# The second half of each turned key page is saved by VectorE instead of ScalarE

## The chip, the cores and the metric

The kernel runs on one core of a Trainium2 chip. The metric is the time of one execution on the device, in microseconds (us); the median of several runs is compared. The core's engines are TensorE (PE in the profile; PEld is its weight load), VectorE (DVE), ScalarE (ACT), GpSimd (POOL) and SyncE (SP). Each has its own instruction queue, works through it in order, and waits on semaphores.

## What is computed

One inference step of a two-layer decoder trunk for a prompt of 256 tokens and 8 sample tokens, which share every weight. Layer 0 mixes by a gated linear recurrence (HGRN2) beside block-sparse attention (MoBA), layer 1 by retention, and a convolutional FFN follows each. The change touches only the sample tokens' attention to their cached keys:

```
def moba_sample(q, k, v, cache_k, cache_v, li, page_table):      # T = 1, D = 128, 8 samples, 8 heads
    k_past = cache_k[li, page_table].reshape(DB, PAST_LEN, H, D)  # 16 pages of 128 keys per sample
    ...
    kmean = mean of k_past over each block of 256 keys
    gate  = q . kmean                                             # the 3 best of 8 blocks are taken
    ...
    s_sel = (q . k of the chosen blocks) * scale
    p     = softmax([s_sel, s_own])
    return p . v of the chosen blocks + p_own . v_own
```

Everything is fp32. The kernel scores every one of the 8 x 16 = 128 key pages, gets each block's gate from the sum of its scores, and masks the blocks that are not chosen.

## The kernel before

**The weight stream.** Almost all of the time TensorE multiplies streamed weights with the 264 activations. Weights come in units of 128 x 512 values in a ring of 8 slots (`raw`). ScalarE makes the rounded high part of a unit (`whi`, line 972 in `hi_unit`), VectorE subtracts it from `raw` for the low part (`wlo`, line 1371 in `lo_unit`), and TensorE makes 12 matmuls of it (lines 565 to 567 in `even_unit`). The slot is 8 units ahead: right after TensorE has finished unit u, ScalarE writes `whi` and then VectorE writes `wlo` for unit u + 8 into the slot that has come free.

**The order of the work.** There is no scheduler. Every engine runs the same written-out loop over tiles n and units k = 0..3 of the first projection. At even k it does the pieces of a table by half tile q = 2n + k/2 (`even_pieces`), then the pages of unit u = 4n + k (`even_pages`), then the unit's own weights. On VectorE the evacuation of a finished tile (`even_evac`, line 1380) stands after the pages of k = 3, and `lo_unit` comes last.

**Key pages.** Units u = 36 to 99 take two key pages each, called page a and page b below. GpSimd loads pages (128 keys x 8 heads x 128) into a ring of four slots (line 1809). TensorE transposes the heads 0 to 3 of a page into PSUM bank `m[0]` and heads 4 to 7 into `m[1]`, four transposes each (line 609); these are the page's half 0 and half 1. ScalarE copies each half, 128 x 512 values, into SBUF (`KT`, line 994), counting `kt_saved` up by one for each. One page later TensorE scores the page from `KT` (line 622). There is one pair of banks, so the transposes of half 0 of the next page wait for the save of half 0 of this one, and those of half 1 for the save of half 1. TensorE's order within a unit is:

```
transposes of page a (half 0, half 1); scores of the page before a
transposes of page b (half 0, half 1); scores of page a
12 matmuls of the unit's weights
```

The table puts other pieces ahead of the two pages, and they fall on the key stage's 64 units like this. On q = 21, 25, ... 49 (k = 2, 8 units) stage 0 of a prompt head: VectorE masks the scores and takes their maxima (lines 1404 to 1414), and ScalarE exponentiates (line 980). On q = 22, 26, ... 46 (k = 0, 7 units) stage 1: VectorE divides (lines 1417 and 1420). On q = 19, 23, ... 47 (k = 2, 8 units) VectorE rotates a key tile (lines 1387, 1388, 1390). On q = 24, 28, ... 48 (k = 0, 7 units) stage 3: TensorE makes the head's output first (lines 598 and 599). The other 34 units, all 32 of odd k and the two of q = 18 and 20, have no such piece.

Of the kernel before, what the change touches and what calls it, by code (L numbers as in the profile page):

```python
# [36 lines left out]
ACT = mybir.ActivationFunctionType  # L37
# [45 lines left out]
N_PAGES = HEADS * PAGES  # L83
# [37 lines left out]
def keys_at(u):  # L121

    r = 2 * (u - 2 * KEY_Q0)
    return range(max(0, r), min(N_PAGES, r + 2)) if r >= 0 else range(0)


def values_at(u):

    def upto(w):
        return min(N_PAGES, max(0, (w - VALUE_U0) * N_PAGES // (VALUE_U1 - VALUE_U0)))  # L130
    return range(upto(u), upto(u + 1))


def key_page(idx):

    return idx // 32, idx // 4 % DEC, idx % 4
# [47 lines left out]
def hybrid_step(nc, x_in, vecs, conv_state, w_even_in, w_even_out, w_odd_in, w_odd_out, w_f0_in, w_f0_o0, w_f0_o1,  # L184
# [4 lines left out]
    with ctx:  # L189
# [3 lines left out]
        def sem(name):  # L193
            return ctx.enter_context(nc.semaphore(name))
# [21 lines left out]
        with ExitStack() as part:  # L216
# [42 lines left out]
            with ExitStack() as sub:  # L259
                def sa(name, shape, dt=F32):  # L260
                    return sb(name, shape, dt, sub)
                zq = sa("zq", [P, HEADS, TOK])
                KT = sa("KT", [P, 2, HEADS, P])
# [79 lines left out]
        m = [ctx.enter_context(nc.psum_tensor(f"mix{n}", [P, 512], F32)) for n in range(6)]  # L343
# [55 lines left out]
        split_order = list(range(HEADS, MT)) + list(range(HEADS))  # L399
        page_landed = [sem(f"page_landed{n}") for n in range(4)]  # L400
        qz_cleared, qz_ready, pz_cleared, masks_set = sem("qz_cleared"), sem("qz_ready"), sem("pz_cleared"), sem("masks_set")
        kt_turned, kt_saved, k_scored, s_saved, s_max = sem("kt_turned"), sem("kt_saved"), sem("k_scored"), sem("s_saved"), sem("s_max")
        pt_turned, pz_saved, v_used = sem("pt_turned"), sem("pz_saved"), sem("v_used")
        kv_stored = sem("kv_stored")
        x_back = sem("x_back")
# [103 lines left out]
        def _(pe):  # L509
# [92 lines left out]
            def key_turn(idx):  # L602

                pe.wait_ge(page_landed[idx % 4], 16 * (idx // 4 + 1))
                for half in range(2):
                    if idx:
                        pe.wait_ge(kt_saved, 2 * (idx - 1) + half + 1)
                    for h in range(4):
                        ins = tr(m[half][:, h * P:(h + 1) * P], ring[:, idx % 4, (4 * half + h) * P:(4 * half + h + 1) * P], ident[:, :])  # L609
                    ins.then_inc(kt_turned, 1)  # L610

            def key_score(idx):

                grp, b, gi = key_page(idx)
                pe.wait_ge(kt_saved, 2 * idx + 2)
                if idx == 0:
                    pe.wait_ge(qz_ready, 1)
                if idx % 32 == 0 and grp:
                    pe.wait_ge(s_saved, 2 * grp)
                for r in range(2):  # L620
                    for j in range(4):
                        ins = mm(m[2][32 * j:32 * j + 32, gi * P:(gi + 1) * P], qz[:, b, r, j, :], KT[:, idx % 2, j + 4 * r, :],  # L622
                                 start=(idx % 32 == 0 and r == 0), stop=(idx % 32 == 31 and r == 1), tile_position=(0, 32 * j),
                                 skip_group_check=True)
                ins.then_inc(k_scored, 1)

            def own_scores():
                pe.wait_ge(AV.sem, AV.at("qk", HEADS - 1))
                pe.wait_ge(kt_saved, 2 * N_PAGES)
                mm(m[0][:, 511:512], qkz[:, :], ones[:, 0:1], start=True, stop=True).then_inc(SP_.sem, SP_.one("own"))  # L630

            def turn_weights(g):
# [31 lines left out]
            def core(h, stage):  # L664
                if stage == 1:
# [24 lines left out]
                    ins.then_inc(CP.sem, CP.one("edges"))  # L690
                    pe.wait_ge(CV.sem, CV.at("va", h))
                    if h == 0:
                        pe.wait_ge(kt_saved, 2 * N_PAGES)
                    else:
                        pe.wait_ge(CA.sem, CA.at("s1", h - 1))
                    for c in range(2):
# [30 lines left out]
            def even_pieces(q):  # L727
                t, a, g = rope_at(q), attention_at(q), gates_at(q)
                if t is not None:
                    rope(t)  # L730
                if a:
                    attention(*a)
                if q == SELECT_Q0:
                    own_scores()
                if q == SELECT_Q0 + 4:
                    turn_weights(0)
                if g and g[0]:
                    core(g[0] - 1, g[1])

            def even_pages(u):  # L740
                for idx in keys_at(u):
                    key_turn(idx)
                    if idx:
                        key_score(idx - 1)
                    if idx == N_PAGES - 1:
                        key_score(idx)
                for v in values_at(u):
                    value_page(v)
# [100 lines left out]
            for s in range(5):  # L849
                core(HEADS - 1, s)  # L850
# [44 lines left out]
        def _(act):  # L895
            A = nc.scalar.activation
# [92 lines left out]
            def key_save(idx):  # L989
                if idx >= 2:  # L990
                    act.wait_ge(k_scored, idx - 1)
                for half in range(2):
                    act.wait_ge(kt_turned, 2 * idx + half + 1)
                    A(KT[:, idx % 2, 4 * half:4 * half + 4, :], m[half][:, :].rearrange("p (h t) -> p h t", h=4), ACT.Copy)\
                        .then_inc(kt_saved, 1)

            def save_scores(grp):

# [104 lines left out]
            def even_pages(u):  # L1103
                for idx in keys_at(u):
                    key_save(idx)
                    if idx % 32 == 0 and idx:
                        save_scores(idx // 32 - 1)
                    if idx == N_PAGES - 1:
                        save_scores(N_PAGES // 32 - 1)
# [145 lines left out]
        def _(dve):  # L1255
            v = nc.vector
# [142 lines left out]
            def attention(h, stage):  # L1399
# [15 lines left out]
                elif stage == 1:  # L1415
# [3 lines left out]
                    for k, (a, b) in enumerate(((0, P), (P, 384))):  # L1419
                        v.tensor_scalar(sm[:, a:b], sm[:, a:b], rl[:, k:k + 1], None, ALU.mult).then_inc(AV.sem, AV.one(f"p{k}"))  # L1420

            def block_max(grp):
                dve.wait_ge(s_saved, 2 * grp + 2)
                v.tensor_reduce(bm[:, 2 * grp:2 * grp + 2], S_all[:, 2 * grp * SPAN:(2 * grp + 2) * SPAN].rearrange("p (j t) -> p j t", t=SPAN),
                                AX_X, ALU.max).then_inc(s_max, 1)
# [43 lines left out]
            def place_weights(g):  # L1469

                if g == 0:
                    dve.wait_ge(pz_cleared, 2)
                dve.wait_ge(pt_turned, g + 1)
                if g >= 2:
                    dve.wait_ge(v_used, DEC * (g - 1))
                v.tensor_copy(picked(PZ[:, g % 2, 0:1], 0, (130, DEC), (32, 4), (1, 2)),
                              picked(m[0][:, 0:1], (g % 2) * P, (2, DEC), (32, 4), (1, 2))).then_inc(pz_saved, 1)
# [101 lines left out]
            def even_pieces(q):  # L1579
                t, a, g = rope_at(q), attention_at(q), gates_at(q)  # L1580
                if t is not None:
                    rope(t)
                    if t == HEADS - 1:
                        place_queries()
                if a:
                    attention(*a)
                if q == 2 * HEADS:
                    for r in range(4):
                        for k in range(4):
                            v.memset(quad[32 * r:32 * r + 32, k:k + 1], float(k == r)).then_inc(masks_set, 1)  # L1590
                if q == SELECT_Q0:
                    block_max(3)
                    select_blocks()
                if q == SELECT_Q0 + 3:
                    normalize()
                if q == SELECT_Q0 + 4:
                    place_weights(0)
                if g:
                    if g[0]:
                        core(g[0] - 1, g[1])  # L1600
                    if g[0] < HEADS:
                        gates(*g)

            def even_pages(u):
                for idx in keys_at(u):
                    if idx % 32 == 2 and idx > 2:
                        block_max(idx // 32 - 1)
                for w in values_at(u):
                    if w % DEC == 0 and w < N_PAGES - DEC:
                        place_weights(w // DEC + 1)  # L1610
# [92 lines left out]
            for n in range(ZE):  # L1703
                for k in range(4):
                    if k % 2 == 0:
                        even_pieces(2 * n + k // 2)
                    even_pages(4 * n + k)
                    if k == 3:
                        even_evac(n)
                    lo_unit(n + 2, k)  # L1710
# [269 lines left out]
```

## Time and profile before

| | |
|---|---|
| median of 3 runs | 3118.78 us (3116.75 to 3128.24) |
| the profiled execution | 3121.49 us, its span 3119.6 us |
| TensorE busy | 2972.8 us, 95% of the span |
| VectorE busy | 1847.3 us, 59% |
| ScalarE busy | 1595.7 us, 51% |
| first to last start of a key-page transpose | 92.5 to 437.5 us |

The span runs from the first to the last instruction of the profiled execution. The busy time of TensorE overlaps itself, since matmuls are pipelined, so its idle time is better read from the waits and from the distances of starts in the timeline. Starts in the timeline are in us from the span's start, and a row can join several instructions of one line (x8).

### The profile page before, as it was taken

To read this page: it belongs to the slowest core of one execution; us is meant where nothing else is said; L and a number is where in the kernel's file an instruction comes from. 1 tells how busy PE (TensorE), PEld (TensorE's weight loads), DVE (VectorE), ACT (ScalarE), POOL (GpSimd) and SP (SyncE) were. 2 spreads that over 40 slices of the span, in tenths; PEclk is the share of its full clock that TensorE was granted. 3 is DMA by queue.
4 is the path that set the end of the run, shared out by engine and by line. 5 is a ranking of instruction groups with operands and counts; after the bars stand their busy time and mean duration, and the time that the engine had idled before them with its cause. 6 is when DMAs were issued, how large, how long until landed. Compare 5 with 4: busy or idle time off the path is not lost.

```text
span 3119.6 us, 73932 instructions
## 1 busy us (share of the span) xinstructions
PE 2972.8 (95%) x26198; PEld 2783.9 (89%) x26198; DVE 1847.3 (59%) x3773; ACT 1595.7 (51%) x3038; POOL 154.2 (5%) x305
## 2 busy tenths in 40 slices
PE   7999999999899999999999999999699999999997
PEld 6877786676799999999999998889599999999997
DVE  5322245555666677657656666666567677657656
ACT  4555563333457755545545454445457755545444
POOL 1111111222000000000000000000000000000000
PEclk9999999999899999999999999999799999999999
DMA  5777768988455555555556565556355555555554
GB/s 198 234 239 240 249 233 283 335 308 320 143 183 174 181 186 178 183 180 181 186 169 200 187 224 209 188 204 223 129 175 174 176 188 182 182 182 180 186 167 139
DMA packets 181710, 630.15 MB, mean 202 GB/s; under 512 B 19553, under 2 KB 40497, under 8 KB 177057
## 3 DMA queue, kind: packets, MB, share of 16 engines
q1 hardware_dynamic: 131744, 442.98, 43.1%
q0 software_dynamic: 38000, 138.35, 13.0%
q10 hardware_dynamic: 11792, 46.48, 4.1%
q8 instruction: 113, 1.85, 0.2%
q14 instruction: 61, 0.49, 0.1%
HBM read 599.00 MB, written 28.73 MB: 201 GB/s over the span
## 4 chain that ended last, share of the span: by engine, by line
PE 85%; DVE 5%; DMA 3%; issue 3%; ACT 2%; POOLq 0%; ACTq 0%; DVEq 0%; SPq 0%; POOL 0%
PE stream L527 21%; PE stream L528 21%; PE stream L529 21%; PE mix L609 4%; PE stream L565 3%; DMA ring<-in_cache_v 3%; PE stream L566 3%; PE stream L567 3%; PE mix L622 2%; PE mix L651 2%; DVE wlo L1265 1%; PE mix L823 1%; PE mix L830 1%; PE mix L720 0%; DVE r L1636 0%
## 5 line engine op out<-in xcount | busy, mean ns | idle before, releaser
L910 ACT ACTIVATE whi<-raw 128x512 fp32r<-128x512 f32 (+1 forms) x1472 | 883.7, 619 | 778.2 <-PE stream L529 767.2
L1265 DVE TENSOR_TENSOR wlo<-raw,whi 128x512 fp32r<-128x512 f32 (+1 forms) x1464 | 951.7, 677 | 494.2 <-ACT whi L910 482.5
L527 PE MATMUL stream<-hB_hi,whi 128*128 128x264 f32 x2816 | 800.2, 284 | 2.5 <-DVE ab L1323 2.5
L528 PE MATMUL stream<-hB_lo,whi 128*128 128x264 f32 x2816 | 798.5, 284 | 0.0
L529 PE MATMUL stream<-hB_hi,wlo 128*128 128x264 f32 x2816 | 798.1, 283 | 0.0
L527 PE MATMUL stream<-hA_hi,whi 128*128 128x264 f32 x1792 | 518.2, 289 | 22.3 <-issue 11.7
L527 PEld LDWEIGHTS stream<-hB_hi,whi 128*128 128x128 f32 x2816 | 531.1, 189 | 3.0 <-DVE wlo L1265 2.9
L528 PEld LDWEIGHTS stream<-hB_lo,whi 128*128 128x128 f32 x2816 | 531.3, 189 | 0.1
L529 PEld LDWEIGHTS stream<-hB_hi,wlo 128*128 128x128 f32 x2816 | 528.7, 188 | 0.0
L528 PE MATMUL stream<-hA_lo,whi 128*128 128x264 f32 x1792 | 510.5, 285 | 0.0
L529 PE MATMUL stream<-hA_hi,wlo 128*128 128x264 f32 x1792 | 510.0, 285 | 0.0
L527 PEld LDWEIGHTS stream<-hA_hi,whi 128*128 128x128 f32 x1792 | 340.4, 190 | 35.9 <-issue 30.9
L1371 DVE TENSOR_TENSOR wlo<-raw,whi 128x512 fp32r<-128x512 f32 x232 | 159.1, 691 | 351.7 <-ACT whi L972 342.6
L528 PEld LDWEIGHTS stream<-hA_lo,whi 128*128 128x128 f32 x1792 | 340.6, 190 | 0.5
L529 PEld LDWEIGHTS stream<-hA_hi,wlo 128*128 128x128 f32 x1792 | 338.7, 189 | 0.0
L972 ACT ACTIVATE whi<-raw 128x512 fp32r<-128x512 f32 x224 | 139.6, 629 | 317.0 <-PE stream L567 316.5
L565 PE MATMUL stream<-hA_hi,whi 128*128 128x264 f32 x896 | 281.5, 314 | 15.8 <-DVE wlo L1371 15.8
L566 PE MATMUL stream<-hA_lo,whi 128*128 128x264 f32 x896 | 261.3, 292 | 0.0
L567 PE MATMUL stream<-hA_hi,wlo 128*128 128x264 f32 x896 | 260.6, 291 | 0.0
L527 PE MATMUL stream<-hid_hi,whi 128*128 128x264 f32 x896 | 254.2, 284 | 0.0
L529 PE MATMUL stream<-hid_hi,wlo 128*128 128x264 f32 x896 | 253.9, 283 | 0.0
L528 PE MATMUL stream<-hid_lo,whi 128*128 128x264 f32 x896 | 253.8, 283 | 0.0
(310 smaller groups left out, 3941.8 us busy)
## 6 DMA issues: line engine op xcount, KB each, us to landing
raw<-in_w_f_in SPq DMA_DIRECT2D x352, 512.0 KB, 3.5
ring<-in_cache_k POOLq DMA_DIRECT2D x128, 512.0 KB, 4.7
ring<-in_cache_v POOLq DMA_DIRECT2D x128, 512.0 KB, 5.7
raw<-in_w_f_o SPq DMA_DIRECT2D x128, 512.0 KB, 3.4
raw<-in_w_odd_in SPq DMA_DIRECT2D x128, 512.0 KB, 3.9
raw<-in_w_even_in SPq DMA_DIRECT2D x112, 512.0 KB, 4.9
raw<-in_w_f_o SPq DMA_DIRECT2D x64, 384.0 KB, 3.5
raw<-in_w_even_out SPq DMA_DIRECT2D x32, 512.0 KB, 3.8
```

The costliest lines, as they stand in the source:

```text
L527: mm(bank, hi, p.src[0][:, kt, :], start=first, stop=False)
L528: mm(bank, hi, p.src[1][:, kt, :], start=False, stop=False)
L529: ins = mm(bank, lo, p.src[0][:, kt, :], start=False, stop=last)
L565: mm(bank, hi, hA[0][:, kt, :], start=(kt == 0), stop=False)
L566: mm(bank, hi, hA[1][:, kt, :], start=False, stop=False)
L567: ins = mm(bank, lo, hA[0][:, kt, :], start=False, stop=(kt == MT - 1))
L609: ins = tr(m[half][:, h * P:(h + 1) * P], ring[:, idx % 4, (4 * half + h) * P:(4 * half + h + 1) * P], ident[:, :])
L622: ins = mm(m[2][32 * j:32 * j + 32, gi * P:(gi + 1) * P], qz[:, b, r, j, :], KT[:, idx % 2, j + 4 * r, :], start=(idx % 32 == 0 and r == 0 ...
L910: A(whi[:, 4 * j + k, 0:n], raw[:, 4 * j + k, 0:n], ACT.Copy).then_inc(hi_done, 1)
L972: A(whi[:, s, :], raw[:, s, :], ACT.Copy).then_inc(hi_done, 1)
L1265: v.tensor_tensor(wlo[:, 4 * j + k, 0:n], raw[:, 4 * j + k, 0:n], whi[:, 4 * j + k, 0:n].bitcast(F32), ALU.subtract).then_inc(lo_done, 1)
L1371: v.tensor_tensor(wlo[:, s, :], raw[:, s, :], whi[:, s, :].bitcast(F32), ALU.subtract).then_inc(lo_done, 1)
```

## The change

The save of half 1 of each page moves from ScalarE's queue to VectorE's. It gets its own semaphore, `kt_halved`. TensorE's transposes of half 0 wait for `kt_saved` and those of half 1 for `kt_halved`; the scores wait for both. On VectorE the new `key_save` stands in `even_pages`, so behind the pieces of the table and behind `lo_unit` of the unit before.

```diff
@@ TensorE, key_turn and key_score
                     if idx:
-                        pe.wait_ge(kt_saved, 2 * (idx - 1) + half + 1)
+                        pe.wait_ge((kt_saved, kt_halved)[half], idx)
...
-                pe.wait_ge(kt_saved, 2 * idx + 2)
+                pe.wait_ge(kt_saved, idx + 1)
+                pe.wait_ge(kt_halved, idx + 1)
@@ ScalarE, key_save
-                for half in range(2):
-                    act.wait_ge(kt_turned, 2 * idx + half + 1)
-                    A(KT[:, idx % 2, 4 * half:4 * half + 4, :], m[half][:, :].rearrange("p (h t) -> p h t", h=4), ACT.Copy)\
-                        .then_inc(kt_saved, 1)
+                act.wait_ge(kt_turned, 2 * idx + 1)
+                A(KT[:, idx % 2, 0:4, :], m[0][:, :].rearrange("p (h t) -> p h t", h=4), ACT.Copy).then_inc(kt_saved, 1)
@@ VectorE
+            def key_save(idx):
+                if idx >= 2:
+                    dve.wait_ge(k_scored, idx - 1)
+                dve.wait_ge(kt_turned, 2 * idx + 2)
+                v.tensor_copy(KT[:, idx % 2, 4:8, :], m[1][:, :].rearrange("p (h t) -> p h t", h=4)).then_inc(kt_halved, 1)
...
                 for idx in keys_at(u):
+                    key_save(idx)
                     if idx % 32 == 2 and idx > 2:
                         block_max(idx // 32 - 1)
```

Two single waits for the last page (in `own_scores` and in the first `core`) are rewritten for the new counts.

VectorE's queue from the evacuation of a tile (zk) over a head's stage 1 (L1417, L1420) to the rotation (L1387) reads like this before:

```order
L1380 TENSOR_TENSOR zk<-stream,rstd 128x264 [waits unit_used]
L1371 TENSOR_TENSOR wlo<-raw,whi 128x512 [waits hi_done]
L1417 RECIPROCAL rl<-lsum 128x2 [waits attn_scalar]
L1420 TENSOR_SCALAR sm<-sm,rl 128x128 [waits attn_vector]
L1420 TENSOR_SCALAR sm<-sm,rl 128x256
L1371 TENSOR_TENSOR wlo<-raw,whi 128x512 [waits hi_done] x2
L1387 TENSOR_TENSOR rt<-zk,ropeb 32x264 [waits tile_free,rope_vector,rope_swapped]
```

and like this with the change, where the same lines have the numbers 1379, 1370, 1416, 1419 and 1386, and L1425 is the new copy:

```order
L1379 TENSOR_TENSOR zk<-stream,rstd 128x264 [waits unit_used]
L1370 TENSOR_TENSOR wlo<-raw,whi 128x512 [waits hi_done]
L1416 RECIPROCAL rl<-lsum 128x2 [waits attn_scalar]
L1419 TENSOR_SCALAR sm<-sm,rl 128x128 [waits attn_vector]
L1419 TENSOR_SCALAR sm<-sm,rl 128x256
L1425 COPY KT<-mix 128x512 [waits kt_turned,k_scored] x2
L1370 TENSOR_TENSOR wlo<-raw,whi 128x512 [waits hi_done]
L1425 COPY KT<-mix 128x512 [waits kt_turned,k_scored] x2
L1370 TENSOR_TENSOR wlo<-raw,whi 128x512 [waits hi_done]
L1386 TENSOR_TENSOR rt<-zk,ropeb 32x264 [waits tile_free,rope_vector,rope_swapped]
```

Two copies stand in each unit between what the table puts there and the unit's `wlo`; the copy of a unit's page a is directly behind the `wlo` of the unit before, or behind that `wlo` and the table's pieces.

TensorE's queue has the same instructions as before; what they wait for changes. One page with the change (L609 the transposes, L623 the scores):

```order
L609 MATMUL mix<-ident,ring 128x128 [waits kt_saved,page_landed3]
L609 MATMUL mix<-ident,ring 128x128 x3
L609 MATMUL mix<-ident,ring 128x128 [waits kt_halved]
L609 MATMUL mix<-ident,ring 128x128 x3
L623 MATMUL mix<-KT,qz 32x128 [waits kt_halved,kt_saved]
L623 MATMUL mix<-KT,qz 32x128 x7
```

The fifth transpose of a page waits for VectorE's queue now, where it waited for ScalarE's.

## Rows read from the trace of the kernel before

**Rows 1.** The page: the span, and busy time of each engine.
```profile
span 3119.6 us, 73932 instructions
...
PE 2972.8 (95%) x26198; PEld 2783.9 (89%) x26198; DVE 1847.3 (59%) x3773; ACT 1595.7 (51%) x3038; POOL 154.2 (5%) x305
```

**Rows 2.** Windows, key stage: PE, PEld, DVE, ACT, POOL busy; granted clock, DMA share, GB/s.
```profile
90.00:440.00 350.00, 331.76 (x3971) 277.06 (x3970) 79.92 (x182) 194.25 (x390) 69.95 (x131) 0.97 0.76 247
```

**Rows 3.** Waits in 95 to 440: us in total, times, longest.
```profile
PE mix L609 <- ACT KT L994: 17.5, 8, 2.2
...
ACT sm L980 <- DVE nmx L1414: 12.8, 8, 1.6
```

**Rows 4.** Groups by form: count, busy us, mean ns.
```profile
L994 ACT ACTIVATE KT<-mix 128x512 f32<-128x512 f32 x256 | 138.2, 590 | 29.5 <-PE mix L609 28.7
...
L1476 DVE COPY PZ<-mix 128x64 f32<-128x64 f32 x16 | 3.5, 217 | 0.0
...
L1668 DVE TENSOR_SCALAR r<-mix 128x264 f32<-128x264 f32 x8 | 3.5, 433 | 9.8 <-PE mix L811 9.8
```

**Rows 5.** Timeline, the unit at 217.06: start, length, engine.
```profile
217.06 1.03 PE L609 MATMUL mix<-ident,ring 128*128 128x128 f32 x8
...
217.86 1.06 ACT L994 ACTIVATE KT<-mix 128x512 f32<-128x512 f32 x2
217.99 0.69 DVE L1371 TENSOR_TENSOR wlo<-raw,whi 128x512 fp32r<-128x512 f32 x1 [7.19 <-ACT whi L972]
...
218.60 1.09 PE L609 MATMUL mix<-ident,ring 128*128 128x128 f32 x8
...
219.21 0.49 PE L609 MATMUL mix<-ident,ring 128*128 128x128 f32 x3
```

**Rows 6.** Timeline, the next unit, with a head's stage 1.
```profile
221.76 1.04 PE L609 MATMUL mix<-ident,ring 128*128 128x128 f32 x8
...
222.63 0.69 DVE L1371 TENSOR_TENSOR wlo<-raw,whi 128x512 fp32r<-128x512 f32 x1 [0.23 <-ACT whi L972]
...
223.43 0.55 DVE L1420 TENSOR_SCALAR sm<-sm,rl 128x128 f32<-128x128 f32 x2
```

**Rows 7.** Timeline, the unit at 232.19, with a rotation.
```profile
232.02 0.69 DVE L1371 TENSOR_TENSOR wlo<-raw,whi 128x512 fp32r<-128x512 f32 x1 [3.95 <-ACT whi L972]
...
232.19 1.04 PE L609 MATMUL mix<-ident,ring 128*128 128x128 f32 x8
...
232.63 0.42 DVE L1387 TENSOR_TENSOR rt<-zk,ropeb 32x264 f32<-32x264 f32 x1
...
233.42 0.42 DVE L1390 TENSOR_TENSOR zk<-rt 32x264 f32<-32x264 f32 x1
```

**Rows 8.** Timeline, the unit at 242.23, with a head's stage 3.
```profile
242.23 1.04 PE L609 MATMUL mix<-ident,ring 128*128 128x128 f32 x8
...
242.44 0.69 DVE L1371 TENSOR_TENSOR wlo<-raw,whi 128x512 fp32r<-128x512 f32 x1 [0.23 <-ACT whi L972]
```

**Rows 9.** Timeline, the unit at 208.65, with a head's stage 0.
```profile
208.65 1.04 PE L609 MATMUL mix<-ident,ring 128*128 128x128 f32 x8
...
210.63 0.17 DVE L1414 TENSOR_SCALAR nmx<-mx 128x2 f32<-128x2 f32 x1
...
211.73 1.06 ACT L994 ACTIVATE KT<-mix 128x512 f32<-128x512 f32 x2
...
212.44 1.09 PE L609 MATMUL mix<-ident,ring 128*128 128x128 f32 x8 [2.19 <-ACT KT L994]
```

**Rows 10.** Windows (columns as in Rows 2), and one timeline row of TensorE.
```profile
150.00:200.00 50.00, 47.78 (x577) 39.77 (x577) 11.88 (x26) 28.61 (x59) 9.68 (x18) 0.97 0.74 242
168.98:172.39 3.41, 3.41 (x28) 2.67 (x27) 0.00 (x0) 1.19 (x2) 0.54 (x1) 0.50 0.49 173
515.00:518.00 3.00, 2.04 (x21) 1.42 (x20) 2.38 (x9) 0.63 (x1) 1.07 (x2) 1.00 0.99 360
...
516.94 0.64 PE L651 MATMUL mix<-ring,PZ 128*32 128x256 f32 x8 [0.96 <-DMA ring<-in_cache_v]
```

More of the change, by code:

```diff
@@ L401, in hybrid_step @@
         qz_cleared, qz_ready, pz_cleared, masks_set = sem("qz_cleared"), sem("qz_ready"), sem("pz_cleared"), sem("masks_set")
-        kt_turned, kt_saved, k_scored, s_saved, s_max = sem("kt_turned"), sem("kt_saved"), sem("k_scored"), sem("s_saved"), sem("s_max")
+        kt_turned, kt_saved, kt_halved, k_scored, s_saved, s_max = sem("kt_turned"), sem("kt_saved"), sem("kt_halved"), sem("k_scored"), sem("s_saved"), sem("s_max")
         pt_turned, pz_saved, v_used = sem("pt_turned"), sem("pz_saved"), sem("v_used")
@@ L628, in own_scores @@
                 pe.wait_ge(AV.sem, AV.at("qk", HEADS - 1))
-                pe.wait_ge(kt_saved, 2 * N_PAGES)
+                pe.wait_ge(kt_saved, N_PAGES)
                 mm(m[0][:, 511:512], qkz[:, :], ones[:, 0:1], start=True, stop=True).then_inc(SP_.sem, SP_.one("own"))
@@ L692, in core @@
                     if h == 0:
-                        pe.wait_ge(kt_saved, 2 * N_PAGES)
+                        pe.wait_ge(kt_halved, N_PAGES)
                     else:
```

## The prediction

> **What bounds the kernel now.** I read the page's first part first: TensorE is busy for 95% of the span, VectorE for 59%, ScalarE for 51% [rows 1]. So TensorE's queue is the clock of the kernel, and an edit elsewhere counts only where TensorE waits for it. Then the window of the key stage: of 350 us VectorE is busy for 79.9 and ScalarE for 194.3 [rows 2]. VectorE has plenty of room on average, but an average says nothing on whether it is free at the moment that a half page is ready. Third, the waits of the key stage. TensorE's transposes wait for ScalarE's save (L994) for 17.5 us in 8 waits, of up to 2.2 us; ScalarE in turn waits 12.8 us, 8 times, for the negated maxima (nmx) of a prompt head [rows 3]. The 8 waits are the 8 units with a head's stage 0, and there are no others of note: in the other 56 units ScalarE's saves are just in time. The timeline shows how closely.
>
> **One unit, as it is.** All times are from T, the start of page a's transposes. In the unit at T = 217.06 the saves of page a start at +0.80 (217.86), two in 1.06, so they end at +1.86 with the second about 0.59 long [rows 4, 5]. Page b's transposes start at +1.54 (218.60). Its last three start at 219.21 and take 0.49 together, of which 0.27 is the last one's own length, so one follows another every 0.11; the fifth, the first of half 1, therefore starts one step before 219.21, at 219.10 or +2.04 [rows 5]. From a save's end to the transposes that it lets go I take 0.12: in the unit at 208.65 the first save ends at 211.73 + 0.59 = 212.32, and the transposes start at 212.44 [rows 4, 9]. So half 1 of page a has to be saved by 2.04 - 0.12 = +1.92. ScalarE makes that by 0.06. The next unit begins at +4.70 (221.76), nowhere near anybody's limit, so within a unit only this one deadline can be missed: page b's saves have until the next unit.
>
> **What the new copy costs by itself.** No copy of 128x512 from PSUM by VectorE is in the trace. From PSUM a copy of 64 columns takes 0.217 us and a one-source operation on 264 columns 0.433 [rows 4]. That is 1.08 ns a column, and 0.217 + 448 x 1.08 ns = 0.70; one cycle a column at the slope of 1.04 gives 0.68. I take 0.69, which is also what a two-source operation of this size takes (L1371) [rows 5]. If the copy ran at half that slope it would be 0.47; two PSUM operations that lie on the full slope speak against it. I keep 0.47 and 0.70 as ends.
>
> The Trainium skill ("VectorE: DVE Perf Modes", section "The TRN2 errata") gives a PSUM-to-SBUF operation on VectorE as (120 + columns) cycles at 0.96 GHz, 0.66 us here as an estimate, and on ScalarE as (172 + columns) at 1.2 GHz, 0.57; the trace's 0.59 agrees with the latter. By that page the move makes the copy itself dearer, and the sum below would be about 18.5 us instead of 20.0.
>
> **Where it stands.** The copy of page a is behind the `wlo` of the unit before, which can't begin before TensorE has finished that unit and ScalarE has made `whi`. So VectorE is held by `wlo` just when half 1 is ready. On VectorE the next instruction starts 0.61 after the start of an L1371 (232.02 to 232.63) [rows 7].
> - *34 units without a piece.* `wlo` at +0.93, copy at +1.54, its end at +2.23, fifth transpose at +2.35 instead of +2.04 [rows 5]: 0.31 late, 34 x 0.31 = 10.5 us.
> - *7 units with stage 1.* The two L1420 run from 223.43 for 0.55, to +2.22, and the copy behind them, which may overlap the last by 0.08, starts at about +2.17, ends at +2.86, and lets the transpose go at +2.98 [rows 6]: 0.95 late, 6.6 us.
> - *8 units with a rotation.* L1390 starts at 233.42, +1.23 of T = 232.19, for 0.42; with the overlap the copy starts at +1.57, the transpose at +2.38 [rows 7]: 0.35 late, 2.8 us.
> - *7 units with stage 3.* TensorE makes the head's output first, so `wlo` starts at +0.21 and VectorE is free at +0.82, before the half is ready; half 1 is there by +1.27 at the latest, when ScalarE begins it in the plain unit (217.86 + 1.06 - 0.59), and 1.27 + 0.69 + 0.12 = 2.08 is at most 0.04 late [rows 5, 8]: nothing.
> - *8 units with stage 0.* VectorE ends its maxima at 210.63 + 0.17, +2.15, and then copies half 1 until about +2.8; ScalarE saves half 0 only at 211.73, +3.08, behind its exponentials, and lets page b go at +3.79 [rows 9]. Half 1 is early now, but half 0 holds the transposes as before: nothing.
>
> ScalarE loses 128 copies of 0.59, 76 us of busy time [rows 4], and none of it was on the path: its first save in a unit starts when `whi` is done, and its `whi` waits for TensorE. Nor does VectorE's own `wlo` come later, since page b's copy is over long before the unit's matmuls are. Page a's late transposes push everything behind them: the scores, the unit's matmuls, the next page's load. Each unit begins when the one before has ended, so the delays add up. The second wait ahead of the scores I cost at nothing, since it is long fulfilled when TensorE comes to it, as the page's landing is ahead of each first transpose; if TensorE's queue lost half the 0.11 between two transposes on it, that would be an estimated 0.05 us a page, 6.4 us.
>
> Sum: 10.5 + 6.6 + 2.8 = **20 us**. The profiled execution took 3121.5 us around a span of 3119.6 and would become 3141.5. It is 2.7 us above the median of 3118.8, and against that median I expect **3139 us**.
>
> **The clock.** In 150 to 200 us the mean granted clock is 0.97: one stretch of 3.41 us at 0.50, that is 1.2 instead of 2.4 GHz, follows the 2 us stop of a stage 0 unit [rows 10]. Six of the seven 50 us windows from 100 to 450 read 0.97, so six of the eight stops have such a stretch, and it costs at most half its length, 1.7 us. A stop of 0.96 us at 516.94 left the clock at 1.00 [rows 10], so stops of 0.3 to 0.95 should not add any. The eight large stops stay and only shift: between -3.4 and +3.4 us from luck.
>
> **The rivals.**
> - *The copy is quick* (0.47 us). Then the 34 units lose 0.09, stage 1 0.73, the rotation 0.13: 3.1 + 5.1 + 1.0 = 9 us, 3128. Against it the slope of rows 4. Chance 0.10.
> - *The loss is covered.* TensorE could have slack between page b's halves that the timeline doesn't show, or the hand-over from VectorE could be quicker than 0.12. If it were 0.04 the first and third case lose 0.08 less each and the second too: 20 - 49 x 0.08 = 16 us, and with a stretch or two of full clock regained it falls within 0.5%, near 3132. Chance 0.14.
> - *Faster.* ScalarE's queue is what TensorE waits for, and it gets shorter. If the relief reached the eight stops whole, 17.5 us would go [rows 3], and the time would be 3101. It decides whether half 0's save can start earlier at a stage 0 unit. It is not behind other saves there but behind the exponentials, which wait for VectorE (12.8 us) [rows 3, 9]; and to gain anywhere else VectorE would have to start its copy before +1.23, while `wlo` holds it until +1.54. Chance 0.03.
> - *Clearly slower still.* The second wait costs its 6.4 us, or a stage 1 stop joined to the next unit's pauses is enough for more stretches at the low clock, 7 x 1.7 = 12 us at most. That gives 3145 to 3151. Chance 0.13.
> - *The forecast.* Chance 0.60, its own range 3134 to 3145.
>
> **How the numbers follow.** About 0.5% (15.6 us) is what a measurement of this kernel can tell from no change, so the line is at 3134.4. The forecast's own lower edge lies on it: of its 0.60 I give 0.05 to "same". Slower: 0.55 + 0.13 and 0.04 of the covered case, 0.72. Same: 0.05 + 0.10 of the quick copy + 0.09 of the covered case, 0.24. Faster: 0.03 and the last 0.01 of the covered case, 0.04. The range reaches down to between the quick copy and the covered case, 3126, and up to 3151.
>
> **What the profile after would show.** VectorE copies KT<-mix 128x512 128 times at 0.68 to 0.70 us, 88 us more busy time, ScalarE 128 fewer. A unit of odd k is 5.01 us instead of 4.70 from T to T, with the copy at +1.54 and the fifth transpose at +2.35; a stage 1 unit has a stop of nearly 1 us that ends with VectorE's copy. First to last transpose takes 20 us longer, and nothing after it changes but by a shift. TensorE's wait for VectorE at L609 comes up 49 times with 15 to 20 us in all, and the 8 waits for ScalarE stay at about 2.2. I am wrong if the copy is much shorter than 0.6 us, if it starts ahead of +1.5 in plain units, or if the stage after the keys, whose pages are loaded ahead, takes the delay up.

## The result and the profile after

The changed kernel takes 3131.89 us (median of 18 runs, 3125.38 to 3134.53), the kernel before in the same sessions 3119.76 us (18 runs, 3112.31 to 3131.93). The ratio of the runs (which is not the quotient of the two medians, 1.0039) is 1.0033 with a 95% interval of 1.0024 to 1.0042: 10 us slower, with 7.5 to 13.1 as the ends, where 20 us were forecast. It is slower beyond doubt, and smaller than the 0.5% that I had called "slower".

The page of the kernel after; the profiled execution took 3127.93 us.

```profile
span 3126.1 us, 74182 instructions
...
PE 2974.6 (95%) x26198; PEld 2774.5 (89%) x26198; DVE 1930.4 (62%) x3901; ACT 1533.8 (49%) x2910; POOL 154.9 (5%) x305
```

Against [rows 1] VectorE is busy 83 us more and ScalarE 62 us less; I had said 88 and 76. Busy time counts an overlap once: before, 256 saves of 590 ns made 138.2 us [rows 4], since a pair of them took 1.06 us [rows 5], and a copy of VectorE's starts some 0.08 us before the instruction ahead of it ends (222.24 against 221.63 + 0.69 below). The groups of the key stage, with the busy time and the mean of one in ns:

```profile
L1425 DVE COPY KT<-mix 128x512 f32<-128x512 f32 x127 | 87.3, 688 | 64.4 <-PE mix L609 64.4
...
L994 ACT ACTIVATE KT<-mix 128x512 f32<-128x512 f32 x127 | 75.0, 590 | 58.6 <-PE mix L609 57.9
```

VectorE's copy of 128x512 from PSUM takes 0.688 us, where 0.69 was worked out from smaller ones [rows 4]; ScalarE's takes 0.590 in both kernels. The waits of the key stage (us in total, times, longest):

```profile
PEld mix L609 <- DVE KT L1425: 19.9, 49, 0.9
PE mix L609 <- ACT KT L994: 17.5, 8, 2.2
...
PE mix L609 <- DVE KT L1425: 5.2, 8, 0.7
```

The first row is new: 49 waits of TensorE's weight loads at the transposes for VectorE's copy. The last one has 8 of the same stops, the longest, as TensorE's matmuls show them; the two rows overlap and are not added. The second is the wait for ScalarE at the 8 units with stage 0, as in [rows 3] to the tenth.

The plain unit, to be laid beside [rows 5]. The row of two shows the end of the fifth transpose's wait:

```profile
220.71 1.04 PE L609 MATMUL mix<-ident,ring 128*128 128x128 f32 x8
...
221.63 0.69 DVE L1370 TENSOR_TENSOR wlo<-raw,whi 128x512 fp32r<-128x512 f32 x1 [2.19 <-ACT whi L973]
...
222.24 0.68 DVE L1425 COPY KT<-mix 128x512 f32<-128x512 f32 x1
...
222.25 1.39 PE L609 MATMUL mix<-ident,ring 128*128 128x128 f32 x8
...
222.98 0.44 PE L609 MATMUL mix<-ident,ring 128*128 128x128 f32 x2
...
225.71 1.04 PE L609 MATMUL mix<-ident,ring 128*128 128x128 f32 x8
```

From T = 220.71: the subtraction (L1370) at +0.92, the copy (L1425) at +1.53, the fifth transpose at 222.98, +2.27 instead of +2.04, and the next unit at 225.71, +5.00 instead of +4.70. It is this next unit that has the head's stage 1 ([rows 6] before):

```profile
227.38 0.55 DVE L1419 TENSOR_SCALAR sm<-sm,rl 128x128 f32<-128x128 f32 x2
227.84 0.68 DVE L1425 COPY KT<-mix 128x512 f32<-128x512 f32 x1
...
228.58 0.66 PE L609 MATMUL mix<-ident,ring 128*128 128x128 f32 x4 [0.67 <-DVE KT L1425]
...
231.30 1.03 PE L609 MATMUL mix<-ident,ring 128*128 128x128 f32 x8
```

The copy starts behind the two L1419, at +2.13, the fifth transpose follows at +2.87 after a stop of matmuls of 0.67 us, and the unit takes 5.59 us instead of 4.70. A unit with stage 0 ([rows 9] before):

```profile
213.78 1.04 PE L609 MATMUL mix<-ident,ring 128*128 128x128 f32 x8
...
217.58 1.06 PE L609 MATMUL mix<-ident,ring 128*128 128x128 f32 x8 [2.19 <-ACT KT L994]
...
220.71 0.38 PE L609 MATMUL mix<-ident,ring 128*128 128x128 f32 x2
```

Page b's transposes start at +3.80, as before; the unit takes 6.93 us. The one at 208.65 in the kernel before took 8.41, from [rows 9] to the unit of [rows 5], since the clock fell behind its stop. So something is gained here. The windows (the third number from the end is the granted clock):

```profile
150.00:200.00 50.00, 46.63 (x557) 37.63 (x558) 22.52 (x42) 18.79 (x39) 9.91 (x19) 1.00 0.75 240
200.00:250.00 50.00, 46.73 (x559) 37.92 (x559) 22.45 (x42) 18.24 (x35) 9.51 (x18) 1.00 0.72 235
250.00:300.00 50.00, 46.65 (x559) 37.66 (x558) 22.52 (x42) 18.93 (x39) 9.96 (x19) 1.00 0.72 238
300.00:350.00 50.00, 46.74 (x534) 37.88 (x533) 20.74 (x40) 17.23 (x33) 9.47 (x18) 0.97 0.69 229
```

Three of them are at the full clock, where 150 to 200 read 0.97 before [rows 10]. Between 100 and 450 us only the last of these has a stretch at 1.2 GHz. And the line of all transposes, with first and last start:

```profile
L609 PE MATMUL mix<-ident,ring x1024: 270/273/405, 92.4 to 449.2; 128*128 128x128 f32 x171
```

From first to last start 356.8 us, where it was 344.9: 11.9 us more for the key stage.

The spans of the two profiled executions are only 6.5 us apart (3126.1 and 3119.6), so outside the key stage this pair differs by 5.4 the other way, 5.1 of it behind the stage. The granted clock accounts for that: added up over windows of 1 us, TensorE stood at 1.2 GHz for 131 us behind the key stage in the kernel before and for 121 in the changed one, and half of the difference is 5 us. The rest of the kernel is only shifted in this pair.

All executions together show the two parts. A stretch of 3.4 us at 1.2 GHz cost 1.5 us above, nearly half its length, so the span times (1 - mean granted clock) is an estimate of what the low clock costs in one execution. Over the 18 of the changed kernel the mean of that is 67.6 us, and 3061.3 are left; over the 57 of the kernel before that ran beside the experiments below it is 75.1, and 3041.6 are left. So the changed kernel loses 19.7 us in work and waiting and 7.5 us less to the low clock. The medians of 18 runs are 12.1 us apart and the ratio stands for 10.3; single executions of the kernel before spread over some 20 us.

### The profile page after: what moved, and what is told of

Its sections match the earlier page's. It is cut to its first block, busy times and chain, and to the rows that moved or that the text cites. A ratio compares the mean times of both kernels' runs of the same rounds, so it can differ in the third digit from the quotient of the medians.

```text
span 3126.1 us, 74182 instructions
## 1 busy us (share of the span) xinstructions
PE 2974.6 (95%) x26198; PEld 2774.5 (89%) x26198; DVE 1930.4 (62%) x3901; ACT 1533.8 (49%) x2910; POOL 154.9 (5%) x305
## 4 chain that ended last, share of the span: by engine, by line
PE 82%; DVE 7%; DMA 4%; issue 4%; ACT 3%; ACTq 0%; POOLq 0%; DVEq 0%; SPq 0%; POOL 0%
PE stream L527 21%; PE stream L528 21%; PE stream L529 21%; DMA ring<-in_cache_v 4%; PE stream L565 3%; PE stream L567 3%; PE stream L566 3%; PE mix L609 2%; PE mix L652 1%; PE mix L623 1%; DVE KT L1425 1%; ACT whi L973 1%; DVE wlo L1264 1%; DVE wlo L1370 1%; PE mix L824 1%
## 5 line engine op out<-in xcount | busy, mean ns | idle before, releaser
L1370 DVE TENSOR_TENSOR wlo<-raw,whi 128x512 fp32r<-128x512 f32 x232 | 159.1, 691 | 244.2 <-ACT whi L973 235.3
```

The source lines that it names most:

```text
L1370: v.tensor_tensor(wlo[:, s, :], raw[:, s, :], whi[:, s, :].bitcast(F32), ALU.subtract).then_inc(lo_done, 1)
```

## The experiments

Each ran beside the kernel before; ratios are to that kernel in the same session and have a 95% interval. Its median was 3118.03 us beside runs 1 to 4, 3119.71 beside 5 to 8 and 3119.52 beside 9 and 10, so rows are compared by their ratios and not by their medians. "Key stage" is the time from first to last start of a transpose (L609) in the profile, from starts read to 0.01 us. "Low" is how many of the eight units with stage 0 had a stretch of 3.4 us at 1.2 GHz behind their stop; in runs 2, 3 and 10 they have no stop of 2.2 us any more, and in run 8 one of 1.29.

| run | median us (runs) | ratio | key stage us | low |
|---|---|---|---|---|
| before | 3119.76 (18) | 1 | 344.9 | 6 |
| the change | 3131.89 (18) | 1.0033 (1.0024 to 1.0042) | 356.8 | 1 |
| 1 VectorE's copy first | 3115.05 (11) | 0.9991 (0.9982 to 1.0000) | 345.5 | 6 |
| 2 before, ScalarE's saves first | 3089.50 (4) | 0.9908 (0.9894 to 0.9922) | 318.0 | 0 |
| 3 the change, ScalarE's saves first | 3116.27 (11) | 0.9994 (0.9985 to 1.0003) | 344.4 | 0 |
| 4 page b only | 3117.37 (12) | 0.9997 (0.9987 to 1.0007) | 345.2 | 6 |
| 5 before once more | 3121.24 (1) | | 345.0 | 6 |
| 6 the change once more | 3126.02 (1) | | 358.6 | 2 |
| 7 page a only | 3132.43 (6) | 1.0041 (1.0027 to 1.0054) | 360.0 | 3 |
| 8 halves swapped | 3148.24 (4) | 1.0091 (1.0077 to 1.0106) | 376.2 | 0 |
| 9 stage 1 behind the copy | 3125.00 (12) | 1.0019 (1.0008 to 1.0030) | 352.3 | 1 |
| 10 both orders | 3103.36 (6) | 0.9945 (0.9926 to 0.9964) | 325.1 | 0 |

The theory: the copy is late because of its place in VectorE's queue, page a's half 1 misses a deadline by 0.2 to 0.9 us in the 49 units that the prediction names, and all of that reaches the end; but fewer low-clock stretches behind the stops of stage 0 give part of it back. The rivals: a copy by VectorE costs TensorE something wherever it stands; or late transposes are worth only half in time.

**1. VectorE's copy of page a ahead of the subtraction.**

```diff
@@ VectorE, even_pages: what is saved early is left out
-                    key_save(idx)
+                    if idx % 2 or idx == 0 or not early(u):
+                        key_save(idx)
...
                     if k == 3:
                         even_evac(n)
+                    for idx in keys_at(4 * n + k + 1):
+                        if idx % 2 == 0 and idx and early(4 * n + k + 1):   # not in units with stage 0
+                            key_save(idx)
                     lo_unit(n + 2, k)
```

> Both halves still shared between the engines, but VectorE's copy of page a's half 1 stands ahead of the low-part subtraction of the unit before, except in the 8 units with a head's stage 0. If the loss is the copy's place in VectorE's queue, the fifth transpose of page b is back at about +2.0 us from the unit's start, a plain unit is 4.70 us again, VectorE ends almost no wait of the transposes, and the time is that of the kernel before within 0.2% (ratio 0.998 to 1.002). If a copy from PSUM by VectorE costs TensorE something wherever it stands, the plain units stay at 5.0 us and the ratio at 1.003.

The unit with stage 1 in its profile, T = 220.02:

```profile
220.02 1.04 PE L609 MATMUL mix<-ident,ring 128*128 128x128 f32 x8
...
221.16 0.69 DVE L1425 COPY KT<-mix 128x512 f32<-128x512 f32 x1 [0.51 <-PE mix L609]
...
221.56 1.09 PE L609 MATMUL mix<-ident,ring 128*128 128x128 f32 x8
221.77 0.68 DVE L1370 TENSOR_TENSOR wlo<-raw,whi 128x512 fp32r<-128x512 f32 x1
```

The copy starts at +1.14, as soon as half 1 is there (it had waited 0.51 for TensorE), and the subtraction behind it at +1.75. Page b's transposes at +1.54 take 1.09 us for all eight, as in [rows 5], where they took 1.39 with the change in place. Waits of the transposes for VectorE are gone. As many copies on VectorE as in the change, and the loss is gone: it was the place in the queue.

**2 and 3. ScalarE's save of page a ahead of the head's exponentials**, in the kernel before (2) and in the changed one (3), only in the 8 units with stage 0.

```diff
             def attention(h, stage, idx):
                 if stage == 0:
                     ...vtok<-m[4]
+                    key_save(idx)                       # page a's, taken out of even_pages there
                     act.wait_ge(AV.sem, AV.at("negmax", h))
                     ...
```

> The kernel before, with ScalarE's saves of page a ahead of the head's exponentials in the 8 units with stage 0. The 8 stops of 2.2 us should go: a stage 0 unit takes 4.7 us instead of 6.9, 8 x 2.2 = 18 us, and the stretches at the lower clock behind the stops should go with them, up to 9 us more: ratio 0.991 to 0.995. Rival: something else holds those units, then they stay above 6 us and the ratio is near 1.

> The changed kernel with the same edit on ScalarE. If the 20 us of late transposes are whole and the changed kernel got part of them back only from fewer low-clock stretches at the 8 stops, then without stops in either the difference between this and the run before it is the whole of the late transposes: 19 us, plus 8 x 0.8 us in the stage 0 units where VectorE's copy stands behind the maxima (fifth transpose at +2.87 instead of +2.03), 26 us or 0.8%; against the kernel before the ratio is 0.999 to 1.003. If instead the late transposes are worth only half in time, the difference is 10 to 17 us.

A stage 0 unit of run 2:

```profile
202.85 1.04 PE L609 MATMUL mix<-ident,ring 128*128 128x128 f32 x8
...
203.55 1.09 ACT L995 ACTIVATE KT<-mix 128x512 f32<-128x512 f32 x2
...
204.39 1.09 PE L609 MATMUL mix<-ident,ring 128*128 128x128 f32 x8
204.83 0.17 DVE L1416 TENSOR_SCALAR nmx<-mx 128x2 f32<-128x2 f32 x1
205.04 0.40 ACT L981 ACTIVATE sm<-sm,nmx 128x128 f32<-128x128 f32 x1 [0.40 <-DVE nmx L1416]
...
207.54 1.03 PE L609 MATMUL mix<-ident,ring 128*128 128x128 f32 x8
```

From T = 202.85 ScalarE makes the two saves at +0.70 and on, then waits for the maxima (L1416) and exponentiates from 205.04; page b's transposes start at +1.54 and the next unit begins at +4.69, in place of +8.41 or +6.93. The line of all transposes:

```profile
L609 PE MATMUL mix<-ident,ring x1024: 270/273/329, 92.8 to 410.8; 128*128 128x128 f32 x171
```

And the same of run 3, with its waits:

```profile
L609 PE MATMUL mix<-ident,ring x1024: 270/273/330, 92.5 to 437.0; 128*128 128x128 f32 x171
```

```profile
PEld mix L609 <- DVE KT L1427: 26.8, 57, 0.9
...
PE mix L609 <- DVE KT L1427: 10.0, 16, 0.7
```

Run 2's key stage is 26.9 us shorter than before: 8 stops of 2.2 us and six stretches of 1.5. Its ratio of 0.9908 lies just outside the 0.991 to 0.995 that I expected, on the side of more gain. Run 3 fell into its range.

The key stages are 318.0 and 344.4 us: 26.4 apart, with no low-clock stretch in either, and the medians, from one session, are 26.8 us apart (0.9994 / 0.9908 = 1.0087). Expected were 26. So the late transposes are worth their whole length, and the second rival falls: without stops to lose or regain clock at, VectorE's share costs 26 us, of which 8 x 0.84 = 6.7 arise only here, where stage 0 units no longer hide the copy behind the maxima, and 19.7 are the loss of the change.

**4 and 7. Only one page of each unit.** ScalarE saves both halves of the other page.

```diff
                 for idx in keys_at(u):
-                    key_save(idx)
+                    if idx % 2 == 1:      # run 4: page b; run 7 has == 0: page a
+                        key_save(idx)
```

> VectorE copies half 1 of page b alone; page a is saved by ScalarE as before. 64 of the 128 copies are moved, and by the deadlines of the timeline page b's have more than 1 us to spare. Deadline theory: no wait for VectorE at the transposes, ratio 0.998 to 1.002. Cost per moved copy: half of the change's 0.33%, 1.0016 or more, with plain units of 4.85 us.

> VectorE copies half 1 of page a alone, the other 64 copies stay on ScalarE. Deadline theory: all of the loss is page a's, so the waits (49, fifth transpose at +2.27, with stage 1 at +2.87), the 44.8 us between stops and the time are those of the whole change, ratio 1.002 to 1.0045. Cost per moved copy: half, 1.0016.

Both move 64 copies. Page b's cost nothing that can be told (0.9997, key stage 0.3 us longer), page a's cost as much as all 128 (1.0041 against 1.0033, the intervals overlap; three low stretches against one make 3 of the 3.2 us between the key stages). In run 4 every kind of unit is at its length of before; in run 7 plain units take 5.00 us and those with stage 1 5.59. Cost per moved copy is out.

**8. Halves swapped.** VectorE saves half 0, ScalarE half 1.

```diff
@@ ScalarE
-                act.wait_ge(kt_turned, 2 * idx + 1)
-                A(KT[:, idx % 2, 0:4, :], m[0]...).then_inc(kt_saved, 1)
+                act.wait_ge(kt_turned, 2 * idx + 2)
+                A(KT[:, idx % 2, 4:8, :], m[1]...).then_inc(kt_halved, 1)
@@ VectorE
-                dve.wait_ge(kt_turned, 2 * idx + 2)
-                v.tensor_copy(KT[:, idx % 2, 4:8, :], m[1]...).then_inc(kt_halved, 1)
+                dve.wait_ge(kt_turned, 2 * idx + 1)
+                v.tensor_copy(KT[:, idx % 2, 0:4, :], m[0]...).then_inc(kt_saved, 1)
```

> VectorE copies half 0 and ScalarE half 1: as many copies of the same size on each engine as in the change. By the deadlines half 0 has to be there by +1.42 and VectorE ends its copy at +2.15: page b's first transpose moves from +1.54 to about +2.27 and the fifth to +2.7, 0.7 late in 33 plain units and 8 with a rotation, 1.3 in 7 with stage 1, against 0.5 gained in the 8 with stage 0: 33 us before any change in the low-clock stretches, ratio 1.007 to 1.013. Cost per moved copy: as the change, 1.0033.

A plain unit, T = 226.46:

```profile
226.46 1.04 PE L609 MATMUL mix<-ident,ring 128*128 128x128 f32 x8
...
227.99 0.68 DVE L1425 COPY KT<-mix 128x512 f32<-128x512 f32 x1
...
228.82 1.07 PE L609 MATMUL mix<-ident,ring 128*128 128x128 f32 x8 [0.75 <-DVE KT L1425]
```

The copy starts at +1.53 whichever half it is, and now the first of page b's transposes is what it holds, to +2.36. The ratio is 1.0091, 28 us, with a key stage 31.2 us longer. It lies in the range expected, but not all of its parts do: the late transposes are worth about 40 us and not 33 (a plain unit takes 5.50 us, 0.80 more where 0.7 was said), and the six low stretches that are gone give 9 back. The deadline that is missed sets the price, not the number of copies. The first of page b's transposes follows the copy's end (228.67) by 0.15 us here.

**5 and 6. A second profile of both kernels.**

> The kernel before once more, for a second profile. In its first profile six of the eight stops of the key stage are followed by a stretch at the lower clock, and in those of the two kernels whose stage 0 units lie as far apart (VectorE's copy first, and page b only) it is six as well. If the count belongs to the distance of the stops and not to chance, it is 5 to 7 again and the stretch from first to last transpose takes 344 to 346 us. If it is chance, it can be anything from 0 to 8, 1.5 us each.

> The changed kernel once more. It had one stretch of low clock behind eight stops, 44.8 us apart where they are 44.0 or 42.4 us apart before. Distance theory: 0 to 3 again, first to last transpose 355.5 to 360 us. Chance: about as many as in the kernel before on average.

The line of all transposes, of run 5 and then of run 6:

```profile
L609 PE MATMUL mix<-ident,ring x1024: 270/273/421, 92.7 to 437.7; 128*128 128x128 f32 x171
```

```profile
L609 PE MATMUL mix<-ident,ring x1024: 270/273/378, 90.1 to 448.7; 128*128 128x128 f32 x171
```

345.0 us with six low stretches, behind the same six of the eight stops as in the first profile, and 358.6 with two. The counts repeat: 6, 6, 6 and 6 in the four profiles of kernels that leave the distance of the stops alone (before twice, runs 1 and 4), and 1, 2 and 3 in the three that have the whole of the late transposes (the change twice, run 7).

**9. The division of stage 1 behind the copy of page a.**

```diff
@@ VectorE, even_pieces: stage 1 is left out where the unit has pages
-                if a:
+                if a and not (a[1] == 1 and keys_at(2 * q)):
@@ VectorE, even_pages
                     key_save(idx)
+                    a = attention_at(u // 2)
+                    if u % 2 == 0 and idx % 2 == 0 and a and a[1] == 1:
+                        attention(*a)
```

> The changed kernel, with VectorE's division of stage 1 behind the copy of page a instead of ahead of it. Queue theory: the 7 units with stage 1 become like plain ones, copy at +1.48, fifth transpose at +2.2 instead of +2.87, unit 4.95 us instead of 5.59: 7 x 0.65 = 4.5 us less of late transposes. The stops then lie 44.2 us apart, near the kernel before, so more low-clock stretches can take some of it back: ratio to the kernel before 1.001 to 1.004. If stage 1 is not what delays the copy, those units stay at 5.6 us.

The line of all transposes:

```profile
L609 PE MATMUL mix<-ident,ring x1024: 269/273/447, 93.3 to 445.6; 128*128 128x128 f32 x171
```

Units with stage 1 fall from 5.59 to 4.93 us, the key stage from 356.8 to 352.3, 4.5 us less with one low stretch in each, and the ratio from 1.0033 to 1.0019, where the intervals overlap: it is the key stage that shows the gain. The term is as large as it was said to be. The part of the expectation on the clock missed, and I had compared the wrong numbers: two stops are 44.2 us apart here where no low stretch lies between them; before that distance is 42.4, and 44.0 is the one with a stretch in it. So run 9 lies near the changed kernel (44.8) and not near the kernel before, and its one stretch fits that.

**10. Both orders together.**

> VectorE's copy ahead of the subtraction and ScalarE's saves ahead of the exponentials together. If VectorE's share of the saves can't gain anything once it costs nothing, all units but those with stage 0 are at 4.70 us, those with stage 0 at 5.5 (VectorE's copy is behind the maxima there), and the time is 6 us above the run with ScalarE's order alone: ratio 0.991 to 0.995. If two engines saving in parallel help TensorE, it is below 0.990.

The units are as expected: 4.70 us without a piece, 5.52 with stage 0. The key stage is 7.1 us longer than that of run 2. The ratios, 0.9945 against 0.9908, are 11.5 us apart, and their two intervals together leave about 7 us to either side. The low clock explains little of what is left: behind the key stage the profiled execution of run 10 has 30 us more at 1.2 GHz than that of run 2 (134 against 104), worth 15 us, but over all their executions the estimate of its cost is 66.7 us against 64.1, and without it they are 11 us apart. Some 4 us stay unexplained, within those intervals. So no gain from a second engine for the saves is to be seen, and run 2 is the best version found: 0.92% faster than the kernel before, by moving the saves of eight pages (16 copies) on one queue.

## Why the prediction was right, and where it was too large

**What bounds the kernel and the deadline: right.** The half 1 of page a was the only thing late. That the list of waits shows the 49 that were named is partly chance: it covers 95 to 455 us and leaves out the first unit. Over the whole stage they are 50, in all of the 34 + 7 + 8 units that were named and in one of the 7 with stage 3.

**The cost of the copy: right.** 0.688 us against 0.69. The quick copy of 0.47 is out. The estimate of 0.66 worked out from the Trainium skill ("VectorE: DVE Perf Modes", section "The TRN2 errata") is 4% below the measurement.

**The terms of the sum: the sum right within 5%.** Laid side by side unit by unit, from T to T, the two traces give this. The 34 plain units lose 0.30 each (0.31 said), 10.1 us together. Sixteen of them, those with k = 1, take 5.35 to 5.74 us before and not 4.70, and are late by the same 0.30. The units with stage 1 lose 0.78 to 0.90 (0.95), 5.9 us where 6.6 stood: three of them took 4.81 us before, and the recorded start of the copy was a slip, since 2.22 - 0.08 is 2.14 and not 2.17 (measured 2.13). Those with a rotation lose 0.33 (0.35; the unit at T = 237.33 is followed by the one at 242.35 in the trace after, against 232.19 and 236.88), the first of them 0.65, 3.0 us in all. Those with stage 3 lose nothing but for two, with 0.28 and 0.14. The sum is 19.4 us, where 20 stood.

That 0.31 and 0.30 are so close is in part luck, since two errors cancel. The hand-over was quicker than the 0.12 that I took: the copy of the plain unit ends at 222.92 and the fifth transpose starts at 222.98, which is 0.06. The difference doesn't come from the engine that copies. Where ScalarE lets the fifth transpose go, in run 8, it is 0.05 (223.68 to 223.73), and where the first one is held it is 0.12 behind ScalarE [rows 9] and 0.15 behind VectorE (run 8). I had taken the figure of a first transpose for a fifth one. Against that, the sixth transpose follows the held fifth one by 0.16 and not by 0.11 (222.98, 223.14, 223.25 and 223.36, where it was 219.10, 219.21, 219.31 and 219.42 before), so that the fifth is 0.23 late and the last 0.29. Runs 1, 4, 7, 8 and 9 show each of these reasons by taking it away or making it larger, and runs 2 and 3 that the sum arrives whole.

**The clock: the failed term.** The step said "the eight large stops stay and only shift: between -3.4 and +3.4 us from luck". The stops stayed, but the stretches at 1.2 GHz behind them went from six to one. A stage 0 unit with such a stretch takes 8.41 us and one without 6.93, so that is 5 x 1.5 = 7.5 us back. 19.4 - 7.5 = 11.9, which is what the key stage grew by. The allowance of 3.4 us either way, two stretches, was too narrow. It was not luck in the sense of the text either: in two profiles of each kernel it was six and six against one and two, and the mean over all executions has the same 7.5 us. I had seen that only six of eight stops have the stretch, and took it for noise of which the mean doesn't move; and the change moves every one of the stops. Where no low stretch lies between them they are 42.4 us apart in the kernels with six (before, runs 1 and 4) and 44.1 to 45.0 in those with one to three (the change, runs 7 and 9). That the distance is the cause is only argued: no run changed it by itself, the changed kernels also have the short waits for VectorE in between, and I can't say from these runs which distances are good ones. What the text said of short stops held: no low stretch follows the 0.7 us stops of the change and of run 3 in the key stage, nor those of run 8, of up to 1.36 us.

**The chances.** The likeliest case was slower by 0.5 to 0.8% and the measured one is 0.33%, which I had given to "same" with 0.24, for two reasons. The quick copy did not come. The other, the covered case with 0.14, named 3132 by way of a hand-over of 0.04 and a stretch or two of full clock regained. The hand-over was short, but the units lost their 0.30 all the same, and it was five stretches: the time is nearly its number, and only its part on the clock was the cause. The time of 3131.9 lies in the whole range of 3126 to 3151, which holds it thanks to these rivals, and below the forecast's own range, which began at 3134.

**Second wait ahead of the scores: right at nothing.** Run 1 has it too, and its units have the length of before.

## What to carry to other kernels

Before half of a job goes to an engine that seems idle, look at what stands in that engine's queue in the 2 us around the moment when the half is ready, not at its share of busy time. Here it stood behind an instruction that itself waits for the end of the unit before, and moving the copy one place forward removed the whole loss. When the trace shows a stop of 2 us at one engine's queue, ask first what is ahead of the late instruction in that queue: a save behind exponentials that wait for a third engine cost more (26.9 us of the key stage) than everything the change was about, and its cure was to do the saves of eight pages first.

## What was not expected of the hardware

TensorE's clock, as the granted clock of the profiles shows it, falls to 1.2 GHz for 3.4 us behind some stops of 2.2 us and not behind others of the same length, and which ones doesn't look like chance: in two profiles of the kernel before it is the same six of eight. In three profiles with the stops 44.8 us apart instead of 42.4 (the change twice, run 7) it is one to three. Whether the distance is what decides isn't shown. So a small change elsewhere can come with 1.5 us more or less for each such stretch, and here they hid 40% of a loss of 19 us. Behind the key stage there are more such stretches, 104 to 134 us at 1.2 GHz in the profiles of before, after and runs 2 and 10, and their number varies from one execution to the next.
